# Modulation rows computed inside the feed-forwards and the input projection of a two-layer diffusion trunk

## What is computed

```python
def trunk_layer(x, cond, lp, lam_init, cache):
    sh1, sc1, g1, sh2, sc2, g2, sh3, sc3, g3 = jnp.split(cond.astype(x.dtype), N_MOD, -1)
    h = x * (1.0 + sc1) + sh1
    f = swiglu(h, lp['ffn_w_gate'][0], lp['ffn_w_up'][0], lp['ffn_w_down'][0])
    x = layer_norm(ALPHA * x + 0.5 * g1 * f, lp['ln_g'][0], lp['ln_b'][0])
    h = x * (1.0 + sc2) + sh2
    m, new_cache = token_mixer(h, lp, lam_init, cache)
    x = layer_norm(ALPHA * x + g2 * m, lp['ln_g'][1], lp['ln_b'][1])
    h = x * (1.0 + sc3) + sh3
    f = swiglu(h, lp['ffn_w_gate'][1], lp['ffn_w_up'][1], lp['ffn_w_down'][1])
    x = layer_norm(ALPHA * x + 0.5 * g3 * f, lp['ln_g'][2], lp['ln_b'][2])
    return x, new_cache
```

## Time and profile before

| what | value |
|---|---|
| median of three runs | 2276.31 us (2273.07 to 2279.59) |
| profiled execution, its device time | 2282.56 us |
| its span | 2280.8 us |
| mean granted TensorE clock | 0.907 |
| TensorE busy in matmuls | 88% |
| VectorE, ScalarE, GpSimd busy | 49%, 31%, 5% |
| DMA | 274.65 MB, mean 120 GB/s |

### The profile page before, as it was taken

The page is one execution under the profiler, slowest core; times in us unless marked ns, Lnnn a source line. Parts: engine busy times, 40 slices in busy tenths (PEclk is TensorE's granted clock), DMA queues, the critical chain, the costliest instruction groups (busy, mean ns, idle before and its releaser), DMA issues. The chain is left out here.

```text
span 2280.8 us, 36833 instructions
## 1 busy us (share of the span) xinstructions
PE 2007.6 (88%) x15488; PEld 1772.9 (78%) x15488; DVE 1109.6 (49%) x1687; ACT 707.5 (31%) x1155; POOL 120.0 (5%) x104
## 2 busy tenths in 40 slices
PE   5999998996749879999969999899966598899995
PEld 3899994985639759999849999769755596599995
DVE  0434335526784764343453434454377647634345
ACT  1422223335432333222232222143444223422221
POOL 0000001000022010000010000010000410100000
PEclk8899998998569989999969999989976699799998
DMA  7533336331000173333463333453300002733320
GB/s 323 218 127 129 129 122 247 117 123 47 12 1 4 50 273 124 127 115 126 151 241 129 126 129 129 167 202 120 129 6 7 2 4 90 264 129 129 121 100 28
DMA packets 40403, 274.65 MB, mean 120 GB/s; under 512 B 4741, under 2 KB 6549, under 8 KB 8289
## 3 DMA queue, kind: packets, MB, share of 16 engines
q1 hardware_dynamic: 35280, 255.34, 30.9%
q0 software_dynamic: 2400, 11.50, 1.3%
q10 hardware_dynamic: 2608, 6.14, 0.7%
HBM read 269.56 MB, written 3.41 MB: 120 GB/s over the span
## 5 line engine op out<-in xcount | busy, mean ns | idle before, releaser
L1780 DVE TENSOR_TENSOR ring_r<-ring,arena_r 128x1024 fp32r<-128x1024 f32 x280 | 327.6, 1221 | 658.5 <-ACT arena_r L1428 658.3
L854 PE MATMUL bank<-arena_r,ring_r 128*128 128x384 f32 x1728 | 588.0, 340 | 0.0
L850 PE MATMUL bank<-arena_r 128*128 128x384 f32 (+1 forms) x1504 | 520.2, 346 | 17.8 <-DVE arena_r L1800 12.9
L853 PE MATMUL bank<-arena_r 128*128 128x384 f32 x1408 | 476.3, 338 | 0.0
L854 PEld LDWEIGHTS bank<-arena_r,ring_r 128*128 128x128 f32 x1728 | 327.7, 190 | 0.0
L850 PEld LDWEIGHTS bank<-arena_r 128*128 128x128 f32 x1504 | 287.5, 191 | 29.3 <-DVE ring_r L1780 16.6
L896 PE MATMUL bank<-arena_r 128*128 128x512 f32 x1056 | 300.8, 393 | 0.0
L1428 ACT ACTIVATE arena_r<-ring 128x1024 fp32r<-128x1024 f32 x280 | 276.7, 1050 | 43.9 <-PE bank L854 31.0
L1467 ACT ACTIVATE arena<-bank 128x384 f32<-128x384 f32 x88 | 43.3, 492 | 757.5 <-PE bank L854 757.5
L853 PEld LDWEIGHTS bank<-arena_r 128*128 128x128 f32 x1408 | 266.2, 189 | 4.6 <-issue 1.0
L896 PEld LDWEIGHTS bank<-arena_r 128*128 128x128 f32 x1056 | 197.5, 188 | 38.3
(11 more groups left out here) (290 smaller groups left out, 2513.4 us busy)
## 6 DMA issues: line engine op xcount, KB each, us to landing
ring<-weights SPq DMA_DIRECT2D x230, 1024.0 KB, 4.8
ring<-first_ada SPq DMA_DIRECT2D x12, 1024.0 KB, 13.6
lnrow<-ln_in POOLq DMA_DIRECT2D x6, 1024.0 KB, 7.7
const<-consts ACTq DMA_DIRECT2D x1, 2659.0 KB, 13.7
x<-x_in ACTq DMA_DIRECT2D x1, 1536.0 KB, 19.5
y_out<-x SPq DMA_DIRECT2D x3, 512.0 KB, 2.6
rows<-row_in POOLq DMA_DIRECT2D x2, 736.0 KB, 14.5
par<-par_in POOLq DMA_DIRECT2D x2, 626.0 KB, 9.1
```

What stands on the lines that cost most here:

```text
L850: mm = pe.matmul(out, w_h, h_h, start=start, stop=False, skip_group_check=True)
L853: pe.matmul(out, w_h, h_l, start=False, stop=False, skip_group_check=True)
L854: return pe.matmul(out, w_l, h_h, start=False, stop=stop, skip_group_check=True)
L1780: ve.tensor_tensor(low_unit(FIRST[stretch], u), raw, place.bitcast(F32), ALU.subtract).then_inc(w_ready, 1)
```

## The change

The modulation stretches go. The rows of the second modulation of a layer's list (`ada1`) are made inside the first feed-forward, those of the next layer's first one inside the second feed-forward (not in the last layer); both come through a second ring of two slots of 1 MB (`ada_ring`), loaded by ACT. The rows of `ada2` are made inside `project`, their chunks standing between those of `feat` and `tokm` in the main ring. The feed-forward loop is written out. Besides, the order of small matmuls is changed in `scores`, `gla`, `carries`, `gains` and `outer`, so that neighbours lie in different row groups of the array; `carries` and `gains` of both chunks of a group become one call, with one wait where there were two. The bias load and clearing of `gate_row` on GpSimd move from `norm` to `next_gate`, which waits for `spread_gate`. On DVE the wait for the layer's parameters moves from behind the first `norm` to ahead of the first feed-forward.

```diff
+ADA_SLOTS = 2
+HALVES = 2 * N_ADA
+EARLY_HALVES = 4
+def project_stream():
+    out, q = [("feat", 0)], 0
+    for c in range(1, N_FEAT):
+        out.append(("feat", c))
+        if q < 9:
+            out.append(("ada2", q))
+            q += 1
+    for c in range(N_TOKM):
+        out.append(("tokm", c))
+        if q < N_ADA:
+            out.append(("ada2", q))
+            q += 1
+    return out
...
                 @block.tensor
+                    def half_row(j, i, bank, lo):
+                        n = N_ADA * (j // 2) + i // 2
+                        if i % 2 == 0:
+                            pe.wait_ge(ada_arrived[n % ADA_SLOTS], 16 * (n // ADA_SLOTS + 1))
+                        w = ada_ring[:, n % ADA_SLOTS, :].rearrange("p (k n) -> p k n", k=KT)
+                        for k in ROW_ORDER:
+                            rows_at = slice(32 * (k // 2), 32 * (k // 2) + 32)
+                            mm = pe.matmul(bank[rows_at, lo:lo + P], silu_c[:, 2 * (k % 2):2 * (k % 2) + 32],
+                                           w[:, k, P * (i % 2):P * (i % 2) + P], start=(k % 2 == 0), stop=(k % 2 == 1),
+                                           skip_group_check=True)
+                        mm.then_inc(mod_row_mm, 1)
+                    def turn_row(part, to, i):
+                        return pe.matmul(to[:, 2 * i:2 * i + 2], part, sel[:, :, 0], start=True, stop=True,
+                                         skip_group_check=True)
...
-                            if j > 0:
-                                gate_rows(pe, FIRST[f"ada{j}"], range(4 * k, 4 * k + 4))
...
+                        def tile_up(f):
...
+                            if rides and f >= 2:
+                                pe.wait_ge(mod_row_ready, rows0 + f + EARLY_HALVES - 2)
+                                half_row(j, f + EARLY_HALVES - 2, ps[0], TOK)
+                            widen(ps[0], u, gate_mm, fresh=(f == 0))
+                            if rides and f == 1:
+                                for i in range(EARLY_HALVES):
+                                    half_row(j, i, ps[2 + i // 2], P * (i % 2))
+                            if i0 + f > 0:
+                                pe.wait_ge(act_ready, i0 + f)
+                            if rides and f >= 2:
+                                if f == 2:
+                                    for i in range(EARLY_HALVES):
+                                        turn_row(mod_row[:, i * P:i * P + P], ps[1][:, TOK:TOK + 32], i)
+                                elif f + EARLY_HALVES - 3 < 16:
+                                    i = f + EARLY_HALVES - 3
+                                    mm = turn_row(mod_row[:, i * P:i * P + P], ps[1][:, TOK:TOK + 32], i)
+                                    if i == 15:
+                                        mm.then_inc(mods_done, 1)
+                            widen(ps[1], u + 1, up_mm)
...
-                        with pe.Fori(0, (FT - 2) // 4) as r:
-                            for f in range(2, 6):
-                                tile_up(f, 12 * r, 4 * r)
-                                tile_down(f - 1, 12 * r, 4 * r)
+                        for f in range(2, FT):
+                            tile_up(f)
+                            tile_down(f - 1)
...
+                        def row_part(q):
...
+                            for i, k in enumerate(ROW_ORDER):
+                                rows_at = slice(32 * (k // 2), 32 * (k // 2) + 32)
+                                mm = pe.matmul(bank[rows_at, lo:lo + 256], silu_c[:, 2 * (k % 2):2 * (k % 2) + 32],
+                                               ring_tile(n)[:, k, :], start=(k % 2 == 0), stop=(k % 2 == 1),
+                                               skip_group_check=True)
+                        def turn_part(q):
+                            pe.wait_ge(mod_row_ready, rows0 + q + 1)
+                            for i in range(2):
+                                mm = turn_row(mod_part[:, q % 2, i * P:i * P + P], ps[5], 2 * q + i)
...
+                        def token_unit(m):
+                            if m == 0:
+                                pe.wait_ge(cond_ready, 2)
...
+                        for name, c in STREAM:
+                            if name == "feat":
+                                feature_unit(2 * c)
+                                feature_unit(2 * c + 1)
+                            elif name == "tokm":
+                                token_unit(2 * c)
+                                token_unit(2 * c + 1)
+                            else:
+                                if c == 0:
+                                    pe.wait_ge(gate_ready, 8)
+                                row_part(c)
+                                if 1 <= c <= 8:
+                                    turn_part(c - 1)
...
-                            for h in range(HEADS):
-                                for g in range(GROUPS):
+                            for g in range(GROUPS):
+                                for h in range(HEADS):
                                     lo, t = GLA_DK * h, slice(g * P, g * P + P)
...
-                    feed_forward(0)
-                    modulation_rows(pe, 1, FIRST["ada1"])
+                    feed_forward(0, True)
                     pe.wait_ge(par_loaded, 16 * LAYER_DMAS * l + 16 * LAYER_DMAS)
...
-                    modulation_rows(pe, 2, FIRST["ada2"])
                     turn_x(2)
-                    feed_forward(2)
-                    if not last:
-                        modulation_rows(pe, NMIX, FIRST["ada3"])
-                        gate_rows(pe, FIRST["ada3"], range(4 * KT))
+                    feed_forward(2, not last)
...
                 @block.scalar
+                    def load_rows(j, n):
+                        slot = n % ADA_SLOTS
+                        sc.dma_start(ada_ring[:, slot, :], ada_in[l, j // 2, n]).then_inc(ada_arrived[slot], 16)
...
+                        def keep_row(i, bank, lo):
+                            sc.wait_ge(mod_row_mm, products_base(j) + i + 1)
+                            sc.activation(mod_row[:, i * P:i * P + P], bank[:, lo:lo + P], ACT.Copy).then_inc(mod_row_ready, 1)
+                            if i % 2 == 1 and i // 2 + ADA_SLOTS < N_ADA:
+                                load_rows(j, i // 2 + ADA_SLOTS)
...
                 @block.vector
-                        if j > 0:
-                            gate_sums(ve, j, l)
...
+                            if rides and f == 16:
+                                modulation_sums(ve, 1 if j == 0 else 3, ps[1][:, TOK:TOK + 32], b_mod[:, j, :])
...
                     turn_x(0)
-                    feed_forward(0)
+                    ve.wait_ge(par_loaded, 16 * LAYER_DMAS * l + 16 * LAYER_DMAS)
+                    feed_forward(0, True)
                     norm(0)
-                    ve.wait_ge(par_loaded, 16 * LAYER_DMAS * l + 16 * LAYER_DMAS)
-                    modulation_sums(ve, 1, b_mod[:, 0, :])
...
-                    modulation_sums(ve, 2, b_mod[:, 1, :])
                     turn_x(2)
-                    feed_forward(2)
+                    feed_forward(2, not last)
                     norm(2)
-                    if not last:
-                        modulation_sums(ve, NMIX, b_mod[:, 2, :])
-                        gate_sums(ve, NMIX, l)
```

More of the change, by code:

```diff
@@ L470, in trunk_kernel @@
         mod_row_ready = sem("mod_row_ready")
+        ada_arrived = [sem(f"ada_arrived{s}") for s in range(ADA_SLOTS)]
+        gate_part = sem("gate_part")
+        part_turned = sem("part_turned")
         gate_row_ready = sem("gate_row_ready")
@@ L789, in _ @@
                 def _(sp):
-                    chunks = N_CHUNKS - (N_ADA if last else 0)
+                    chunks = N_CHUNKS
                     rounds = chunks // RING
@@ L887, in tile_down @@
-                        def tile_down(f, du, df, first=False, last=False):
-                            hi, lo, free = unit(3 * f + 4 if not last else FFN_UNITS - 1, du)
-                            pe.wait_ge(act_split, df + (i0 + f + 1))
+                            if i0 + f > 0:
+                                pe.wait_ge(silu_done, i0 + f)
+                            if rides and f >= 2:
+                                pe.wait_ge(mod_row_ready, rows0 + f + EARLY_HALVES - 2)
+                                half_row(j, f + EARLY_HALVES - 2, ps[0], TOK)
@@ L891, in tile_down @@
+                            widen(ps[1], u + 1, up_mm)
+                        def tile_down(f):
+                            hi, lo, free = unit(3 * f + 4 if f < FT - 1 else FFN_UNITS - 1)
+                            first, last = f == 0, f == FT - 1
+                            pe.wait_ge(act_split, i0 + f + 1)
+                            if rides and first:
+                                pe.wait_ge(mod_row_ready, rows0 + EARLY_HALVES)
                             for g in range(GROUPS):
```

(29 more changed lines are left out.)

363 lines of the change are left out of this document (201 added, 162 removed).

## The result

The kernel before took 2277.32 us (median of 4 runs beside the changed one, 2273.07 to 2279.59), the changed kernel 2337.24 us (2336.66 to 2339.00). The ratio is 1.0267, with a 95% interval of 1.0249 to 1.0284: 60 us slower. The forecast was 2345 us, slower. The profiled executions have spans of 2280.8 and 2335.3 us, so their difference is 54.5 us.

The account below looks back on a forecast made before the run. TensorE was taken to bound feed-forwards and projection, the layer norm the stretches between sub-layers. 2280.8 us plus 110 added minus 40.5 removed gave a 2350 us span, 2345 on the median's scale; range 2305 to 2385.

Parts of the forecast that it names:

- (a): First feed-forward to projection, twice: 5.0 us gained at the first main matmul plus 1.8 for the slow first weight unit.
- (b): Output projection to second feed-forward, twice: 7.05 us gained less 2.4 for a cold TensorE, 9.3 us in all.
- (c): Layer 0 to layer 1, once: the layer ends with the norm, 8.6 us gained.
- (d): Reordered small matmuls: GLA scores gain 3.0 us per layer, 6 in all; carries and gains 3 us in all.
- A half row's visit: Row products inside the feed-forward rides: 0.46 us of work plus 0.40 us for going in and out.
- A turned row: Two passes without change of mode: 0.25 us each in rides, 0.45 a pair in projections, 19 us in all.
- rival 2: Cheap visits: drain half hidden and freed stages at their upper bounds, net 38 us added, 2315 us; chance 0.2.
- rival 3: Weight loads set the pace of half rows, 0.915 us instead of 0.46, 33 us more, 2378 us; chance 0.15.
- Rival 1: Row products run beside the full-array matmuls, so visits cost next to nothing; 2256 us, faster; chance 0.04.
- rival 4: Projection chunks each land 1 us late, 27 us per layer, so TensorE waits; 2400 us; chance 0.04.
- rival 5: No difference: terms of both sides cancel, said to happen at 0.35 us less for every visit; chance 0.03.
- The waiting sums: In the projection, `token_unit(0)` waits for DVE's two sums with TensorE's `tokm` work behind it: 0.6 us, twice.

Follow-up runs that it names:

- order: Experiment 1: the kernel before with only the change's reordered small matmuls, modulation stages kept; 2271.55 us against 2277.90 beside it, ratio 0.9969.
- experiments 2 to 4: The changed kernel with half rows in two visits (2357.81 us), with four of eight products (2323.38 us), or with products 64 columns wide instead of 128 (2321.56 us).
- experiment 4: The changed kernel with each half-row product 64 columns wide instead of 128, the rest filled by a ScalarE copy; 2321.56 us, ratio to before 1.0192.
- Experiments 6 and 8: 6: the kernel before with reordered small matmuls and modulation stages fitted under the norm, 2252.48 us, ratio 0.9902; 8: `win3`, 2243.34 us.
- win3: `win2` with a filler matmul in each TensorE wait for a row chunk; 2243.34 us, ratio to the kernel before 0.9844.
- win2: The kernel before with reordered small matmuls, modulation stages under the norm, and turned rows in fours between row chunks; 2264.96 us, ratio 0.9943.

## Why the prediction was right

**The bound.** The reading that TensorE is full in feed-forwards and projection, and the norm decides between them, held: both stages still show a full TensorE, and from the first feed-forward's end to the norm's end it is 22.1 us in both kernels.

**(a) to (c), what went.** (a) was 5.0 us at the first main matmul and is 6.2: L994 starts 6.9 us behind the norm's end and takes 6.65 us, where some 8 us from 7.2 on was the estimate. The slow first unit, put at 1.8 us, is inside the projection's change: its first 24 matmuls take 5.85 us in the kernel before and 4.32 in the changed one, so it was 1.5 us. (b) was 7.05 less 2.4 for a cold start: it is 7.3 and 7.4 (5.0 to 7.8 when the same stretches of `order` are the measure), and the feed-forward without rides shows the cold start bare, +2.35. Its first 4 us now run at a granted clock of 0.50 (1.2 GHz) instead of 1.00, while its later tiles take 12.58 us written out as in the loop. (c) was 8.6 and is 8.6. **(d)** was 6 for GLA and is 5.8 with what the next stretch takes back; the 3 us for carries and gains have 2.4 in the ledger, but experiment 1 has 0.8 for them, so this term isn't shown.

**What was added.** A half row's visit was 0.46 + 0.40 = 0.86 us and is 0.79, of which experiments 2 to 4 put 0.45 on streamed columns and 0.34 on the visit: the mechanism and both terms stand, the fixed one between the 0.25 of the interleaved transposes and the 0.40 taken. Its parts were the wrong way round: 0.27 going in and 0.13 going out were taken, while the ride's tile has 0.10 ahead of the first product and some 0.24 behind it. That their sum came near is partly luck. A turned row was 0.25 and is 0.22. Rides with their turned rows were 58 + 12 = 70 us and are 21.4 + 21.1 + (23.5 - 2.35) = 63.7. The projections were 31.6 + 7.2 + 1.2, less the slow units' 3.6, so 36.4, and are 34.2. Both are smaller mostly by the visits' price, 0.06 us less for each of 87. The waiting sums were put at 0.6 us a projection and take 0.5.

**The sum.** On the span's scale 2350 was forecast and 2335.3 came, 15 us less. 8.5 of it is the added side. The other 6.5 is what goes: 2.5 from (a), smaller terms, and 4 us in stretches for which nothing was forecast (2.25 at the program's start and 1.9 in the output projections). The first of these is no more than the scatter between executions, and the second may be. The median came 7.8 us under the forecast, less than the span did: the profiled execution of before had 3.5 us more than its median and that of after 2 us less, and the median of the runs before had been taken 1 us lower. So the near hit of the median is in part luck: the sum itself was 15 us off.

**The rivals.** The tile of 13.6 us lies where the forecast put it (13.7), between the marks 13.0 and 14.1 of rivals 2 and 3. Rival 1 falls by the visit's edges, rival 2 by what was added (101 us with the slow units counted as removed, not 85 to 95, against 46.5 us removed, not 50 to 57), rival 3 by experiment 4, rival 4 by a TensorE that waits 0.5 us in a whole projection, and rival 5 by the time. What "costs nothing" did cost nothing: ACT's silu still waits 805 us in all for TensorE's gate matmuls, which is the cover.

**Slips in the working.** None moves the forecast. Rival 5's condition is wrong: 0.35 us less for each of 87 visits is 30 us and leaves the kernel 39 us slower; to cancel the 69.5 us a visit would have to cost 0.8 us less, nearly all of a half row. The upper bounds of what goes add up to 59, not 57. And the old stages had more than 5 visits: with the gate products between the transposes their trace has 38, which became 87.

**What the prediction didn't see.** It took the exposed part of the old stages as the price to win by moving the products. Experiments 6 and 8 show that most of it could be had, 37 us in all with the GLA order, with the products left where TensorE idles.

## What to carry to other kernels

Before moving work off a stage boundary, ask whether the boundary is long because of that work or because of its order: here a matmul stage hid nearly whole under a norm once its copies, buffers and turned rows were taken in the order in which they became ready. Work on the bounding engine costs its full time inside a dense stretch, and a small matmul of another array form 0.34 us more for each visit, so few long visits beat many short ones. When small matmuls are paced by transfers, try to fill the waits: here a TensorE that waited between them ran them at half clock, and fillers gave the time back.

## What the runs showed of the hardware

- Going from 128x128 matmuls to the 128x32 form and back costs 0.34 us a visit (60 visits, 20.5 us), while a two-column pass in the 128x128 form between the same matmuls costs 0.11 us. So the price goes with the other form, not with the mere interruption.
- A TensorE that is busy in bits can be worse off than one that is busy in full with useless work: `win3` does all of `win2`'s work and 35 more matmuls, and is 22 us faster. Ahead of the first projection its granted clock is 1.00 where `win2` had 0.79, and ahead of the second feed-forward 0.87 where `win2` had 0.60.
- The order of 192 small matmuls of 32 rows halves their busy time, 26.0 to 12.2 us at about half clock, when neighbours go to different row groups.
- Keeping TensorE busy through the norm (clock 1.00) didn't keep its clock through the transposes behind it (0.58 over those 10 us).
